# A hybrid decoder layer on eight cores: set-up transfers merged and queued early, mixer weights loaded ahead, first and last tile in pieces

## The reference, cut to what matters

```
x = x + 0.5 * (silu(h @ wg) * (h @ wu)) @ wd        h = rmsnorm(x), width 1024, d_ff 2816
[q | k | v | u] = rmsnorm(x) @ w_in                 512 | 128 | 128 | 512 columns
attn = banded attention (window 128, a sink and a T5 bias for each head)
y    = gelu(Re(C xs) + D u),  xs[t] = lam_bar * xs[t-1] + B_bar u[t]    (32 groups, 64 complex states)
ssm  = y * sigmoid(y @ w_glu + b_glu)               w_glu 512 x 512
x = x + concat(attn, ssm) @ w_out                   w_out 1024 x 1024
x = x + 0.5 * (silu(h @ wg2) * (h @ wu2)) @ wd2     h = rmsnorm(x)
y = rmsnorm(x)
```

## Time and profile before

| | |
|---|---|
| time, median of three runs (lowest to highest) | 1539.46 us (1401.86 to 1601.07) |
| the profiled execution | 1405.27 us |
| its slowest core, first to last instruction | 1403.7 us (cores: 1386.2 to 1403.7) |
| PE busy | 1263.5 us, 90% of the span, 7678 matmuls |
| DVE / ACT / POOL busy | 672.4 / 390.3 / 126.4 us |
| mean granted TensorE clock, slowest core | 0.956 |
| PE's longest idle stretches | 25.27, 9.77 (at the start), 6.99, 6.14, 5.12, 5.12, 4.86, 4.85, 4.05 us |

### The profile page before, as it was taken

One profiled execution on the slowest core, in us unless ns is written; L12 is line 12 of the kernel. 1 busy time (PEld: TensorE's weight loads), 2 busy tenths in 40 slices (PEclk: granted clock), 3 DMA queues, 4 the chain that ended last, 5 costly groups with the idle time before them and its releaser, 6 DMA issues.

```text
span 1403.7 us, 21425 instructions; the slowest of 8 cores (1386.2 to 1403.7 us)
## 1 busy us (share of the span) xinstructions
PE 1263.5 (90%) x7678; PEld 580.7 (41%) x7678; DVE 672.4 (48%) x1410; ACT 390.3 (28%) x679; POOL 126.4 (9%) x210
## 2 busy tenths in 40 slices
PE   4882899998999999988989899999978899989996
PEld 1331344443445444443435444344433334444443
DVE  3231676645348538823353256568723363222224
ACT  2240322144222342222242213432232332101122
POOL 0210110102000000001120000000001000000000
PEclk9887899999999999999999999999989999999999
DMA  8456464448234334433483233344353349344413
GB/s 190 106 121 148 111 117 89 71 67 106 31 83 83 64 53 84 88 55 61 72 100 50 56 71 65 57 82 92 68 87 56 61 97 181 57 72 76 71 29 120
DMA packets 68279, 117.34 MB, mean 84 GB/s; under 512 B 26504, under 2 KB 32296, under 8 KB 68144
## 3 DMA queue, kind: packets, MB, share of 16 engines
q0 software_dynamic: 43632, 80.79, 36.4%
q1 hardware_dynamic: 24544, 35.19, 8.2%
HBM read 183.39 MB, written 15.37 MB: 142 GB/s over the span
## 4 chain that ended last, share of the span: by engine, by line
PE 72%; DVE 10%; DMA 6%; issue 5%; ACT 4%; SPq 2%; DVEq 0%; POOL 0%; ACTq 0%; POOLq 0%
PE ps L204 66%; PE psy L204 6%; SPq L82 2%; DMA xT_s<-xT 2%; ACT L208 1%; DMA wm_s<-wout 1%; DVE hB_s L214 1%; DVE mix_s L211 1%; ACT rt_s L208 1%; DVE hA_s L214 1%; DVE xT_s L214 1%; DVE hA_s L211 1%; DMA wm_s<-wglu 1%; DMA scr_tab<-hB_s 1%; DVE aT_s L211 1%
## 5 line engine op out<-in xcount | busy, mean ns | idle before, releaser
L204 PE MATMUL ps<-hA_s,wf 128*128 128x512 bf16 x1408 | 328.8, 393 | 43.1 <-ACT sg_s L208 32.3
L204 PE MATMUL ps<-hB_s,wf 128*128 128x512 bf16 (+1 forms) x2112 | 335.6, 319 | 9.6 <-ACT sg_s L208 4.0
L204 PE MATMUL ps<-aT_s,wf 128*128 128x512 bf16 (+1 forms) x1595 | 309.0, 349 | 16.7 <-DVE xT_s L214 14.0
L208 ACT ACTIVATE sg_s<-ps 128x512 f32<-128x512 f32 (+2 forms) x284 | 148.7, 536 | 546.8 <-PE ps L204 473.3
L211 DVE TENSOR_TENSOR aT_s<-ps,sg_s 128x512 bf16<-128x512 f32 (+1 forms) x220 | 130.0, 594 | 328.9 <-PE ps L204 244.8
L214 DVE SCALAR_TENSOR_TENSOR xT_s<-ps,xT_s 128x512 f32<-128x512 f32 (+1 forms) x200 | 116.6, 594 | 252.8 <-PE ps L204 252.5
L204 PEld LDWEIGHTS ps<-hB_s,wf 128*128 128x128 bf16 x2112 | 159.1, 98 | 182.6 <-issue 23.0
L204 PEld LDWEIGHTS ps<-hA_s,wf 128*128 128x128 bf16 x1408 | 139.5, 100 | 226.9 <-issue 75.9
L204 PEld LDWEIGHTS ps<-aT_s,wf 128*128 128x128 bf16 x1595 | 134.5, 99 | 180.0 <-issue 41.4
L82 POOL DMA_DIRECT2D wf<-wgu x88 | 46.9, 533 | 702.2 <-PE ps L204 659.9
L204 PE MATMUL ps<-mix_s,wm_s 128*128 128x512 bf16 (+1 forms) x360 | 75.7, 366 | 25.8 <-DMA wm_s<-wout 12.7
(11 more groups left out here) (166 smaller groups left out, 764.1 us busy)
## 6 DMA issues: line engine op xcount, KB each, us to landing
wf<-wgu POOLq DMA_DIRECT2D x88, 512.0 KB, 5.2
wf<-wd POOLq DMA_DIRECT2D x59, 352.0 KB, 4.4
yT<-xT_s SPq DMA_DIRECT2D x16, 512.0 KB, 4.2
xT_s<-xT SPq DMA_DIRECT2D x4, 1024.0 KB, 12.3
scr_tab<-hB_s SPq DMA_DIRECT2D x8, 512.0 KB, 4.4
hA_s<-scr_tab SPq DMA_DIRECT2D x16, 256.0 KB, 3.6
wm_s<-wout POOLq DMA_DIRECT2D x16, 256.0 KB, 3.8
hB_s<-scr_tab SPq DMA_DIRECT2D x16, 256.0 KB, 3.6
```

Source lines behind the costliest of these rows:

```text
L204: return self.P.op('pe', lambda e: e.matmul(out, lhsT, rhs, start=start, stop=stop, skip_group_check=skip), waits=waits, signal=signal)
L208: return self.P.op('act', lambda e: e.activation(out=out, in_=in_, func=func, **kw), waits=waits)
```

## The change

It has five parts.

1. Start: tile 0 of `xT` comes as two pieces of 256 tokens, each as two transfers of four slabs; tile 1 as two transfers; `wf0` waits for the first transfer, `wf1` for the third, `wf2` for the first half of tile 1. A one-element Ln runs on ACT at the very start. Block 0 of the first stage runs on the two pieces separately, and blocks 1 and 2 run on tile 0 before any group of tile 1.
2. The thirteen set-up inputs are issued on SP directly behind tile 1 of `xT`, and the chain `lam` begins without the four slots of delay.
3. The 32 transfers out of `scr_f` become 4 with the same bytes. The copy into `BT` reads the new layout. Eight DVE instructions of the set-up note 1.1 instead of 0.45.
4. `w_glu` is loaded when the scan of a half starts. The first two slabs of `w_out` go into rows 7 and 6 of the half's `h` buffer, issued before the GLU; slabs 2 and 3 follow into `wm` when the GLU is done.
5. End: tile 3 of `down_last` is done as two pieces of 256 tokens, each with its own norm and output transfers.

```diff
         self.t_norms = P.dma('sp', self.norms[:], d["norms"], self.slot("d_norm"))
+        self.warm = self.act(self.rtt[:, 0:1], self.epst[:, 0:1], AF.Ln, waits=[t_eps])
         tx = []
         for p in range(4):
-            tk = P.dma('sp', self.xT[:, 2 * p:2 * p + 2, 0:512], d["xT"][:, 2 * p:2 * p + 2, 0:512], self.slot("d_x0%d" % p))
-            self.tok_x[(2 * p, 0)] = self.tok_x[(2 * p + 1, 0)] = tk
+            o, k0 = 256 * (p // 2), 4 * (p % 2)
+            tk = P.dma('sp', self.xT[:, k0:k0 + 4, o:o + 256], d["xT"][:, k0:k0 + 4, o:o + 256], self.slot("d_x0%d" % p),
+                       waits=tx[0:1] if p == 2 else [])
             tx.append(tk)
...
-        self.feed.issue(waits=[tx[1]])
-        t1 = P.dma('sp', self.xT[:, :, 512:1024], d["xT"][:, :, 512:1024], self.slot("d_x1"), waits=[tx[3], self.feed.ready[0][1]])
+        self.feed.issue(waits=[tx[0]])
+        self.feed.issue(waits=[tx[2]])
+        for p in range(2):
+            tk = P.dma('sp', self.xT[:, 4 * p:4 * p + 4, 512:1024], d["xT"][:, 4 * p:4 * p + 4, 512:1024], self.slot("d_x1%d" % p),
+                       waits=[tx[3]])
...
+        self.feed.issue(waits=[self.tok_x[(0, 1)]])
...
+        sgen = self.setup_gen()
+        next(sgen)
...
-        self.norm_now(0, 0, 6)
+        self.norm_now(0, 0, 6, 0, 256)
...
-        for st, h, us in self.ffn(0, 0, pre={2: lambda: self.norm_now(0, 1, 7)}):
+        for st, h, us in self.ffn(0, 0, pre={1: self.second_quarter, 3: lambda: self.norm_now(0, 1, 7)}):
...
+    def second_quarter(self):
         for kc in range(KC):
-            self.square(kc, ti, 'dve' if kc % 2 else 'act')
-        for _ in self.norm_fin(gi, ti, bank):
+            self.tok_x[(kc, 0)] = self.x_first[2 + kc // 4]
+        self.norm_now(0, 0, 7, 256, 256)
...
-                order = [(0, 0), (1, 0), (0, 1), (1, 1)] + order[4:]
+                order = [(0, 0, 0, 256), (0, 0, 256, 256), (1, 0, 0, 512), (2, 0, 0, 512), (0, 1, 0, 512), (1, 1, 0, 512),
+                         (2, 1, 0, 512)] + order[6:]
...
-        for k, ti in enumerate((4, 2, 3)):
+        for k, (ti, o, n) in enumerate(((4, 0, 64), (2, 0, 512), (3, 0, 256), (3, 256, 256))):
...
         emit_z(0)
         yield None
+        wg = self.wm[:, :].rearrange("p (k n) -> p k n", k=4)
+        self.t_wglu = P.dma('pool', wg, self.dram["wglu"], self.slot("d_wglu%d" % half), waits=self.mring.free[0] + self.mring.free[1])
...
-        t_w = P.dma('pool', wg, d["wglu"], self.slot("d_wglu%d" % half), waits=self.mring.free[0] + self.mring.free[1])
+        t_w = self.t_wglu
+
+        first = []
+        for c in range(2):
+            k0 = (7 - c) * HLEN[half]
+            dst = w[:, k0:k0 + 1024]
+            fr = [self.ssm_end] + self.tok_y[3] + ([self.att_s] if half == 1 else [])
+            first.append((dst, P.dma('pool', dst, d["wout"][c].rearrange("p k n -> p (k n)"), self.slot("d_wo%d%d" % (half, c)), waits=fr), None))
...
-        for _ in range(4):
-            yield None
+        yield None
...
-        for ty in range(2):
-            for h in range(8):
-                src = _AP(scr_t, (h * 2 + ty) * 256, [[1, 128], [1, 128]])
-                P.dma('sp', stage[:, ty, h, :], src, s_tp, waits=[t_sc])
...
+        P.dma('sp', stage, _AP(scr_t, 0, [[1, 128], [256, 16], [1, 128]]), s_tp, waits=[t_sc])
+        P.dma('sp', stage2, _AP(scr_t, 256, [[1, 128], [512, 8], [1, 4]]), s_tp, waits=[t_sc])
+        for g in range(2):
+            t_tp = P.dma('sp', stage3[64 * g:64 * g + 64], _AP(scr_t, 64 + 2048 * g, [[1, 64], [512, 4], [1, 64]]), s_tp, waits=[t_sc])
...
-                yield 0.45
+                yield 1.1
```

More of the change, by code:

```diff
@@ L554, in final_gen, with final_tile @@
             yield from self.final_tile(ti, 6 + i % 2)
-    def final_tile(self, ti, bank):
-        t0, n = TT[ti]
-        sl = self.slot("d_out%d" % ti)
+    def final_tile(self, ti, bank, o=0, n=None):
+        n = TT[ti][1] if n is None else n
+        t0 = TT[ti][0] + o
+        sl = self.slot("d_out%d%d" % (ti, o))
         kc = 0
-        for c in self.norm_fin(3, ti, bank, final=True):
+        for c in self.norm_fin(3, ti, bank, True, o, n):
             if c is not None:
@@ L573, in ffn @@
             tok_a = {}
-            order = [(jj, ti) for jj in range(NJH) for ti in tiles]
+            order = [(jj, ti, 0, TT[ti][1]) for jj in range(NJH) for ti in tiles]
             if pre is not None and h == 0:
-                order = [(0, 0), (1, 0), (0, 1), (1, 1)] + order[4:]
-            left = {jj: len(tiles) for jj in range(NJH)}
+                order = [(0, 0, 0, 256), (0, 0, 256, 256), (1, 0, 0, 512), (2, 0, 0, 512), (0, 1, 0, 512), (1, 1, 0, 512),
+                         (2, 1, 0, 512)] + order[6:]
+            left = {jj: sum(1 for e in order if e[0] == jj) for jj in range(NJH)}
             wts = {}
-            for idx, (jj, ti) in enumerate(order):
+            for idx, (jj, ti, o, n) in enumerate(order):
                 if jj not in wts:
@@ L1171, in mix_tail @@
             self.h_free[half] = self.h_free[half] + [self.att_s]
-        nxt = self.mring.load(d["wout"][0].rearrange("p k n -> p (k n)"), 1024)
+        rest = [self.mring.load(d["wout"][c].rearrange("p k n -> p (k n)"), 1024) for c in (2, 3)]
         cnt = 0
@@ L1175, in mix_tail @@
         for c in range(KC):
-            wv, t_w, wi = nxt
+            wv, t_w, wi = first[c] if c < 2 else rest.pop(0)
             wv3 = wv.rearrange("p (k n) -> p k n", k=8)
-            if c + 1 < KC:
-                nxt = self.mring.load(d["wout"][c + 1].rearrange("p k n -> p (k n)"), 1024)
             for ti in tiles:
@@ L1199, in mix_tail @@
                 yield 1.75 * n / 512.0
-            self.mring.release(wi, t_y)
+            if wi is not None:
+                self.mring.release(wi, t_y)
+                if c + 2 < KC:
+                    rest.append(self.mring.load(d["wout"][c + 2].rearrange("p k n -> p (k n)"), 1024))
         for a in pend:
```

72 lines of the change are left out of this document (37 added, 35 removed).

## The result

| | before | after |
|---|---|---|
| ratio of times, runs in turn on one chip | 1 | **0.9616**, 95% interval 0.9588 to 0.9645 |
| median of the runs | see below | 1346.89 us (1346.01 to 1350.05, 4 runs) |
| profiled execution | 1405.27 us | 1346.22 us |
| its span; clock of its slowest core | 1403.7 us; 0.956 | 1344.7 us; 0.977 |
| PE busy | 1263.5 us (90%) | 1246.0 us (93%) |

The runs of before fell into two groups (two near 1401 and two at 1539 and above, median 1470.66), so the ratio, and every median further down, is taken from undisturbed runs alone. Against the profiled execution the change took 59.1 us off; the forecast said 62.3, and its 0.956 lies just outside the interval. The sum was nearly right, but two of its terms were not, and it was luck that others made up for them.

A forecast was written before the change was run, and what follows sets the result against it. Bound by PE, busy 90% of the span: only its idle time and slow clock could be had. −7.8 + 3 − 9.9 − 10.6 − 6 − 29 − 2 = −62.3 from 1405.3 gives 1343 us, range 1327 to 1365.

The forecast's parts named there:

- Part 6: Mixer tails: loading `w_glu` and `w_out` ahead removes four PE waits and the slow clock behind them, −29 us.
- Part 4: Sine table wait: 32 transfers out of `scr_f` become 4, PE's idle 25.27 becomes about 14.7, −10.6 us.
- its own 13 us: Sine table: by the Trainium skill's fit, everything up to the table takes 13 us at most; wait some 3 us.
- The rival in which the table is let through at once: Sine table: merged transfers drain faster, the whole 25.27 us wait goes; 1326 us, chance 0.10.
- Parts 1 and 2: Start: new tile and block order, −7.8 us; a `wf` weight buffer wanted earlier, +3 us.
- the start is bound by DMA work: Rival for the start: DMA work, not order, binds it, so the new order only moves waits; 1362 us, chance 0.20.
- Part 2: Start, block 3: `wf0` is needed two groups after its release instead of three, a wait of +3 us.
- Part 3: First pass: set-up inputs queued early remove PE's 6.99 us wait and the half-clock stretch behind it, −9.9 us.
- Part 5: Set-up on DVE: higher notes spread eight instructions, and the stretch falls under stage 'g'; the 5.12 us wait goes, −6 us.
- Part 7: End: the last tile in two pieces shortens the work behind the last addition, with some waits added before, −2 us.
- the rival on the other side: Whole program: a fuller PE is granted a lower clock, slower than before once the mean is below 0.91; chance 0.02.

The follow-up runs named there:

- split32: The changed kernel with the four merged transfers out of `scr_f` put back to the 32 of before; ratio 0.9637 to the kernel before, median 1352.4 us.

## Why the forecast came out as it did, step by step

**Part 6, the bulk (29), was right**: 12.5 us in the first tail and 18.3 in the second, 30.8 together, and 31 when undone. What was counted as half of the busy time at 0.5 was there, and no new wait took its place. That one term is half of the gain.

**Part 4 (10.6) is the first step that failed.** What failed in it was "PE's idle 25.27 becomes about 14.7": it became 21.62, and the gain of 3.8 us lies under the lower end of 6. The mechanism, a queue that has the same bytes to move, was right; the size was not. The interval from `scr_f`'s landing to the table's shrank by 3.8 us (by 3.2 over eight cores). Merging by itself is worth 6.4 in the same surroundings; the other 3 were lost because those surroundings had changed. The same 32 transfers with the same copies took from `scr_f`'s landing to the table's 34.1 us in the kernel before and, by split32's slowest core, 37.4 in the changed one (eight cores: 32.9 and 35.1). I had priced the queue's work by the busy shares of one stretch of before, and had the table land with about half of the weights' work still to come. With the work moved 25 us forward, three loads of `wf`, 512 KB each, are issued between `scr_f` and the table's landing, where it was one of 512 KB and one of 352:

```profile
q1 hardware_dynamic: 5206, 5.09, 46.7%
q0 software_dynamic: 510, 1.83, 32.5%
```

(the change, 74 to 114 us, as long a stretch as that of the earlier trace rows: packets, MB, share of 16 engines' time). The hardware queue has the same 18.7 us of work, the weights have 13.0 instead of 7.4. As an estimate, 78.5 + 18.7 + 13.0 is 110.2, and the table landed at 108.8, with all of the weights' work ahead of it rather than half. That it was these loads fits, but no run takes them away.

By the fit of the Trainium skill (DMA: Bandwidth & Descriptors, Anatomy of one DMA), measured for a transfer issued by POOL, one of 1 MB would take 4.4 us, an estimate; the one out of `scr_f`, issued by SP, landed in 11.7. Following the trace rather than that rule was right; to read the share as a price that would not move was wrong. (By its own 13 us, the prediction's wait by that fit should have been some 4 us, not 3.) The rival in which the table is let through at once (1326) had no support in any run.

**Parts 1 and 2 (7.8 less 3) are the second.** "PE's first group moves to about 14.5" happened on four cores (15.3 to 15.6) and failed on the other four (19.5 to 20.0), and the time is that of the slowest core. The product of the first group on tile 1 started at 54.55 with one group more done, so 51.1 against 49.30: 1.8 us lost, not 4.8 won. What I had not priced: `wf0` is now under way with three pieces of `xT` instead of two, and on the slowest core took 10.9 us from its issue at 8.41, against 7.2 from 10.00. The rival "the start is bound by DMA work" was right about the mechanism, though not about its 1362 us; with the second half of tile 0 held back the first group came at 12.0 to 15.0 us on all cores. Part 2's wait came out as 0.97.

**Part 3 (9.9) was right in size**: 7.9 + 1.8 = 9.7 up to the table wait, and 12 when undone; but of the 12 only 3 lie up to the end of the table wait, so undoing it does not show the wait of 6.99 as the place. **Part 5 (6)**: 5.12 became 0.36, and with the slow clock behind it that makes 7.3 us; but the note, the first of the two reasons given, was not the one. It alone is worth 1 us by ratio, which is within the noise. That the wait went because the stretch came under the first stage is what is left, and was not tried. **Part 7 (2)** gave 1.5 by the table above: 4.1 at the end, less 2.6 for the halves.

What made up for parts 1 and 2 together and part 4, short by 6.6 and 6.8 us, is what I had left out or put too low. That it came to nearly as much is luck. **Before** had a wait at 283 us, the same place of which is at 254 **after** (timelines of PE):

```profile
283.30 0.37 PE L204 MATMUL psy<-mix_s 128*32 128x32 bf16 x32 [2.91 <-DVE mix_s L223]
```
```profile
254.64 0.37 PE L204 MATMUL psy<-mix_s 128*32 128x32 bf16 x32 [0.95 <-DVE mix_s L223]
```

That is 2.0, and 1.7 of slow clock behind it; the wait of 3.38 at 339 became 2.74 (0.6); the tails gave 1.8 more than forecast, part 5 gave 1.3 more, the stretch from the second tail to the last tile 2.7. Less 1.0 for a longer slow clock behind the table, 0.5 for part 7 and 0.2 for part 3, these are 8.4 us, and 62.3 − 13.4 + 8.4 = 57.3. The other 1.7 us of the 59.0 I can't place.

**The clock** rose to 0.977 and did not fall with a fuller PE; the rival on the other side found nothing.

## What to carry to other kernels

A large wait changes what every other part seems to be worth: the new start measured better than the old one with the table's wait and worse without it. So remove the cause of the large wait first (here a condition on when ACT starts its tables, 21 us for one line on the kernel before), then price the rest. A transfer's price depends on the traffic around it, so after a move count again what falls beside it; and look at all cores, since the time is that of the slowest, and a start that is faster on half of them need not help. Loads that can go ahead should: here the idle time was only two thirds of what the late weights cost (20.1 of 31 us).
